# A first norm modulated by columns from strip products, with the load list reordered

## The chip, the cores and the metric

The kernel runs on one core of one Trainium2 chip. The metric is the device time of one execution in microseconds (us). The core has a TensorE (products), a VectorE, a ScalarE and a GpSimd engine, and SyncE, whose queue issues the weight loads. Each runs its own instructions in order and waits on semaphores.

## The reference

One sequence of 256 tokens of width 1024 goes through a first block (a modulated hybrid mixer and a mixture of experts) and then two attention layers. Only the beginning matters here:

```python
c_act = jax.nn.silu(c)
mod = (c_act @ w_mod[l] + b_mod[l])[:, None, :]          # 6 x 1024 columns
sh1, sc1, gt1, sh2, sc2, gt2 = jnp.split(mod, N_MOD, axis=-1)
h = layer_norm(x) * (1.0 + sc1) + sh1
proj = h @ w_in                                           # z, xbc, dt, q, k, v, f, g_ssd, g_att
...
xbc = jax.nn.silu(causal_depthwise_conv(xbc, conv_w, conv_b))
dt = jax.nn.softplus((dt_raw + dt_bias).astype(jnp.float32))
log_f = jax.nn.log_sigmoid((f_raw + forget_b).astype(jnp.float32))
```

All data are f32.

## The kernel before, in words

**Chunks and the ring.** Weights come in chunks of 2 MB (128 partitions x 4096 f32) into a ring of three slots. FIRST_CHUNKS lists the chunks of the first block in the order of their loads, and chunk n of the list has slot n mod 3. SyncE (`load`, line 1179) issues them in that order; ahead of each it waits until the last user of the slot has ended (`used`, set where TensorE's product is written), and everything later in the list stands behind that wait. The list begins mod0, mod2, mod1, mod3, dtf, xbc0, xbc1, xbc2, xbc3, q, k, v, z0, z1, ga0, ga1. dtf is small: 24 columns in two loads, 96 KB.

**Modulation.** mod0 and mod1 are the halves of the shift, mod2 and mod3 those of the scale. `modulation(i)` (line 702) makes rows of 512 columns, the same in all 128 partitions. For mod0 and mod2 (in MOD_SUMMED) VectorE multiplies the chunk's eight parts by c_act and adds them up (`add_modulation`, L1794 and L1796), and one product with ones sums over the partitions (L707). For mod1 and mod3 eight products with a broadcast c_act do it all (L713). The bias is added by a one-row product (L719).

**Norm.** VectorE runs the layer norm on rows (L1684 to L1694), takes the modulation from PSUM (`take_modulation`, L1806), scales and shifts the rows h_rows in two halves (L1699, L1701), and TensorE transposes them (`turn_rows`, L586) into the PSUM banks X and O in turns. ScalarE copies each piece twice (L1401): to h_t in f32 and to first_high, a rounded fp32r. VectorE makes first_low, the difference (L1831).

**Split products.** The chunks in FIRST_SPLIT (xbc0 to xbc3, q, k, v, z0, z1, ga0, ga1) are multiplied as three fp32r passes: high x high, high x low, low x high. For each, ScalarE makes the high part (`make_high`, L1353) once the chunk has landed, and VectorE the low part in place (`make_low`, L1669). TensorE waits for the low part. `product_turned` (L626) gives xbc, q and k in two halves in the banks G0 and G1. ScalarE takes them out (`take_first`, L1339) and then makes the high part of the chunk two further on.

**dtf.** Its plain f32 product (`product_rows`, L611) stands before xbc0's. VectorE and ScalarE compute softplus from it in small steps (L1837 to L1867 on VectorE, L1410 to L1413 on ScalarE), and VectorE makes the low part of xbc1 only after them.

**Order on VectorE after that:** low xbc2, `convolve(0)` (L1881, L1883), low xbc3, `convolve(1)`, low q, `convolve(2)`, low k, low v and so on. On ScalarE the tanh of convolution group i - 1 (`conv_gate`, L1407) follows the high part that is made after xbc i.

## Time and profile before

| what | value |
|---|---|
| three timed runs | 1970.43, 1972.98, 1973.97 us; median 1972.98 |
| the profiled execution | 1971.96 us, its span (first to last instruction) 1970.2 us |
| TensorE products, busy | 1755.8 us, 89% of the span |
| VectorE, ScalarE, GpSimd busy | 853.9, 593.7, 22.6 us |
| TensorE's mean granted clock | 0.932 of full |
| first split product starts | 63.3 us |

Times inside the profile are counted from the first instruction. Engines are PE (TensorE), PEld (its weight loads), DVE (VectorE), ACT (ScalarE), POOL (GpSimd), SP (SyncE), and a name with q is an engine's own queue of issues. L with a number is a line of the kernel, which can be a helper's. In a row of the timeline the first number is the start, the second the time from there to the end of the group, both in us; an entry in brackets says how long the engine was idle before it, and what released it. A plain f32 product is two instructions (passes), an fp32r product one.

### The profile page before, as it was taken

The numbers are of one execution on the slowest core, as the hardware profiler recorded it, in microseconds if no ns is written. First come the engines' busy times: TensorE is split into PE (matmuls) and PEld (weight loads), VectorE is DVE, ScalarE is ACT, GpSimd is POOL, SyncE is SP. The second block draws the span as 40 slices with busy tenths as digits, with TensorE's granted clock in tenths as the row PEclk, the third lists the DMA queues.
The fourth block names the chain that finished last, engine by engine and source line by source line (L and its number), as shares of the span: only waits on it lengthen the run. The fifth ranks groups of instructions, "written<-read, shape, count | busy, mean of one in ns | idle before, by whom it ended". The sixth has DMA issues, their size and how long they took to land.

```text
span 1970.2 us, 21742 instructions
## 1 busy us (share of the span) xinstructions
PE 1755.8 (89%) x9183; PEld 1284.4 (65%) x9183; DVE 853.9 (43%) x1201; ACT 593.7 (30%) x879; POOL 22.6 (1%) x80
## 2 busy tenths in 40 slices
PE   5999899988999959999988779996999989859997
PEld 1997555454434328565677679985756667649995
DVE  4675153243101055353465345534543365434643
ACT  1443210000111123243434234423333533433341
POOL 1000010000000000000000000000000000000000
PEclk9899787988999979999989889997999998979998
DMA  7455222657999964413234135536433232414552
GB/s 242 170 179 201 91 86 85 219 193 292 400 401 405 405 137 165 152 44 128 107 128 171 43 129 172 204 118 151 167 107 110 99 140 105 167 43 154 189 178 90
DMA packets 211212, 333.24 MB, mean 169 GB/s; under 512 B 51251, under 2 KB 102709, under 8 KB 211125
## 3 DMA queue, kind: packets, MB, share of 16 engines
q1 hardware_dynamic: 205312, 325.90, 47.5%
q10 hardware_dynamic: 5814, 6.11, 0.9%
q8 instruction: 65, 1.06, 0.2%
q14 instruction: 21, 0.17, 0.0%
HBM read 330.94 MB, written 1.05 MB: 168 GB/s over the span
## 4 chain that ended last, share of the span: by engine, by line
PE 68%; issue 12%; DVE 8%; DMA 7%; ACT 4%; SPq 1%; POOL 0%; POOLq 0%; DVEq 0%; ACTq 0%
PE ps_g L611 20%; PE ps_g L626 12%; PE ps_g L991 7%; DMA arena<-in_w_up_dram 5%; PE ps_g L911 4%; PE ps_o L681 3%; PE ps_p L611 2%; PE ps_s L611 2%; DMA ring<-in_w_mod_dram 2%; PE ps_p L1128 2%; PE ps_s L1128 2%; PE ps_s L652 1%; DVE ring_r L1669 1%; PE ps_x L586 1%; PE ps_p L671 1%
## 5 line engine op out<-in xcount | busy, mean ns | idle before, releaser
L1669 DVE TENSOR_TENSOR ring_r<-ring,late_w 128x4096 fp32r<-128x4096 f32 (+1 forms) x52 | 225.8, 4343 | 153.5 <-ACT late_w L1353 153.5
L1353 ACT ACTIVATE late_w<-ring 128x4096 fp32r<-128x4096 f32 (+1 forms) x52 | 185.0, 3557 | 234.7 <-PE ps_g L626 111.5
L626 PE MATMUL ps_g<-h_t_r,late_w 128*128 128x256 f32 x768 | 219.0, 285 | 0.0
L626 PE MATMUL ps_g<-hf_high,late_w 128*128 128x256 f32 x704 | 199.0, 283 | 3.8 <-DVE h_t_r L1657 3.8
L626 PE MATMUL ps_g<-hf_high,ring_r 128*128 128x256 f32 x704 | 199.0, 283 | 0.0
L626 PEld LDWEIGHTS ps_g<-h_t_r,late_w 128*128 128x128 f32 x768 | 148.6, 193 | 0.0
L991 PE MATMUL ps_g<-ring,h_t 128*128 128x512 f32 x320 | 145.7, 600 | 0.0
L626 PEld LDWEIGHTS ps_g<-hf_high,late_w 128*128 128x128 f32 x704 | 135.1, 192 | 4.5 <-DVE h_t_r L1657 4.5
L626 PEld LDWEIGHTS ps_g<-hf_high,ring_r 128*128 128x128 f32 x704 | 134.8, 192 | 0.0
L911 PE MATMUL ps_g<-ring,arena 128*64 128x512 f32 x384 | 115.7, 602 | 10.4 <-DMA arena<-in_w_up_dram 8.8
L1339 ACT ACTIVATE arena<-ps_g 128x512 f32<-128x512 f32 (+2 forms) x62 | 35.2, 567 | 219.3 <-PE ps_g L611 145.3
L991 PEld LDWEIGHTS ps_g<-ring,h_t 128*128 128x128 f32 x320 | 58.2, 190 | 63.9 <-issue 62.7
L611 PE MATMUL ps_g<-ring,h_t 128*128 128x512 f32 (+1 forms) x224 | 92.7, 573 | 5.0 <-DVE arena L2031 3.0
L911 PEld LDWEIGHTS ps_g<-ring,arena 128*64 128x64 f32 x384 | 36.5, 139 | 84.1 <-issue 84.1
L1377 ACT ACTIVATE arena<-arena,neg_max 128x256 f32<-128x256 f32 (+1 forms) x160 | 71.3, 448 | 61.0 <-DVE neg_max L1720 61.0
L586 PE MATMUL ps_x<-ident,h_rows 128*128 128x128 f32 x80 | 18.8, 379 | 73.1 <-DVE h_rows L1677 31.5
L611 PE MATMUL ps_g<-ring,arena 128*128 128x512 f32 (+1 forms) x176 | 75.3, 589 | 2.7 <-issue 1.6
L611 PE MATMUL ps_g<-early_w,mix_high 128*128 128x512 f32 (+2 forms) x192 | 72.9, 380 | 5.0 <-issue 5.0
L611 PEld LDWEIGHTS ps_g<-ring,h_t 128*128 128x128 f32 x224 | 43.7, 214 | 49.9 <-issue 48.6
L611 PE MATMUL ps_g<-ring_r,mix_high 128*128 128x512 f32 (+2 forms) x192 | 72.5, 378 | 0.0
L611 PE MATMUL ps_g<-early_w,mix_low 128*128 128x512 f32 (+2 forms) x192 | 72.2, 376 | 0.0
L681 PEld LDWEIGHTS ps_o<-arena 128*128 128x128 f32 x400 | 54.7, 211 | 26.3 <-issue 26.3
(525 smaller groups left out, 3366.6 us busy)
## 6 DMA issues: line engine op xcount, KB each, us to landing
ring<-in_w_in_dram SPq DMA_DIRECT2D x27, 2048.0 KB, 7.8
ring<-in_w_gate_up_dram SPq DMA_DIRECT2D x44, 1024.0 KB, 6.9
ring<-in_w_gate_dram SPq DMA_DIRECT2D x16, 2048.0 KB, 16.5
arena<-in_w_down_dram SPq DMA_DIRECT2D x16, 2048.0 KB, 15.3
ring<-in_w_mod_dram SPq DMA_DIRECT2D x12, 2048.0 KB, 9.4
ring<-in_w_down_dram SPq DMA_DIRECT2D x10, 2048.0 KB, 7.7
ring<-in_w_up_dram SPq DMA_DIRECT2D x8, 2048.0 KB, 18.0
arena<-in_w_up_dram SPq DMA_DIRECT2D x8, 2048.0 KB, 19.3
```

The lines of the kernel that those rows point to most:

```text
L586: ins = pe.transpose(b.ap[0:size, i * SEQ + tb * P:i * SEQ + (tb + 1) * P], piece(tb), ident[:, :])
L611: ins = pe.matmul(b.ap[:, 0:n], x[:, k, tb * P:(tb + 1) * P], a[:, k, lo:lo + n], start=k == 0 and i == 0, stop=k == nk - 1 and i == len(b ...
L626: ins = pe.matmul(b.ap[:, (f % 2) * SEQ:(f % 2 + 1) * SEQ], a[:, k, f * P:(f + 1) * P], x[:, k, :], start=k == 0 and i == 0, stop=k == nk ...
L652: ins = pe.matmul(s4[:, i, 0:nk], q[lo:lo + HD, pair, qb * P:(qb + 1) * P], kk[lo:lo + HD, kpair, 0:nk], start=True, stop=kind != "fox")
L681: ins = pe.matmul(O.ap[:, i * width:(i + 1) * width], probs_t[:, i, b, :], v(step, i, b), start=b == 0, stop=b == kbs - 1)
L911: ins = pe.matmul(b.ap[lanes, :], taken_t[:, k, lanes], w[:, k, :], start=k == 0, stop=k == KD - 1)
L991: ins = pe.matmul(G[tb].ap[:, :], h_t[:, k, tb * P:(tb + 1) * P], w[:, k, :], start=k == 0, stop=k == KD - 1)
L1128: ins = pe.matmul(b.ap[:, half * HALF:(half + 1) * HALF], a[:, k, tb * P:(tb + 1) * P], x[:, k - 4 * c, half * HALF:(half + 1) * HALF], st ...
L1339: act.activation(d, src, func, scale=scale).then_inc(b.free, 1)
L1353: act.activation(high_w[name][:, 0:n], ring[:, slot, 0:n], ACT.Copy).then_inc(high_ready.sem, 1)
L1377: ins = act.activation(s, s, ACT.Exp, bias=neg_max[:, n % 2, i:i + 1], scale=-1.0, accum_out=den[:, n % 4, i:i + 1])
L1669: dve.tensor_tensor(ring_r[:, slot, 0:n], ring[:, slot, 0:n], high_w[name][:, 0:n].bitcast(F32), ALU.subtract).then_inc(low_ready.sem, 1)
```

## The change

The norm's modulation is no longer made as rows. For each of mod0, mod2, mod1 and mod3 eight products (`mod_quarters`) use c_act as a stationary operand of only 32 columns; the product of part k goes to the PSUM partitions of strip k mod 4, so the four strips hold partial sums. ScalarE keeps them in SBUF (`keep_quarters`). One-column products (`mod_columns`) with `quarter`, which has a one in the first partition of each strip, sum the strips and put the result on the partitions; a second one-column product adds the bias. TensorE transposes the normed but unmodulated rows into the banks S and PT, and VectorE scales and shifts them from there into h_t with one instruction for each of eight tiles (`first_columns`). High and low parts of h are made in two halves (`first_rows_high`, `first_rows_low`).

VectorE's sums for mod0 and mod2 are gone. xbc0 is loaded third, ahead of mod1 and mod3; dtf stays sixth in the list. dtf's product goes behind xbc1's, in the banks S and PT; ScalarE's part of softplus goes behind the take of xbc1, and VectorE's behind `convolve(0)`, ahead of the low part of xbc3.

```diff
-MOD_SUMMED = [0, 2, 8, 9, 10, 11]
-FIRST_CHUNKS = (MOD_FIRST + ["dtf"] + [f"xbc{i}" for i in range(4)] + ["q", "k", "v", "z0", "z1", "ga0", "ga1", "mod8", "gs0", "mod9", "att", "gs1",
+MOD_SUMMED = [8, 9, 10, 11]
+FIRST_CHUNKS = (MOD_FIRST[:2] + ["xbc0"] + MOD_FIRST[2:] + ["dtf"] + [f"xbc{i}" for i in range(1, 4)] + ["q", "k", "v", "z0", "z1", "ga0", "ga1", "mod8", "gs0", "mod9", "att", "gs1",
                 "mod4", "so0", "so1", "mod10", "mod5", "o0", "o1", "mod11", "mod6", "mod7"])
...
-        ASIDE = ("bra1", "brb1", "brc1", "out1", "memv", "xo1")
-
-        MOD_ORDER = range(len(MOD_FIRST))
+        ASIDE = ("dtf", "bra1", "brb1", "brc1", "out1", "memv", "xo1")
 
...
-            return (S, PT) if part == "layer" and tag in ASIDE else G
+            return (S, PT) if tag in ASIDE else G
...
-            for i in MOD_ORDER:
-                modulation(i)
+            def mod_quarters(j):
+
+                name, b = MOD_FIRST[j], G[j % 2]
+                w = keys(chunk(pe, "first", name), KD, HALF)
+                claim(b, name)
+                for k in range(KD):
+                    lanes = slice(32 * (k % 4), 32 * (k % 4) + 32)
+                    ins = pe.matmul(b.ap[lanes, :], c_act[:, k:k + 1].broadcast_to([P, 32]), w[:, k, :], start=k < 4, stop=k >= 4)
+                ins.then_inc(b.full, 1)
+                used["first", name] = (b, name)
+
+            def mod_columns(j):
+
+                b, (at_b, name) = G[j % 2], ((X, "mod_left") if j < 2 else (O, "mod_right"))
+                i = int(MOD_FIRST[j][3:])
+                pe.wait_ge(b.free, b.nth("first", MOD_FIRST[j]))
+                if j % 2 == 0:
+                    claim(at_b, name)
+                for k in range(4):
+                    col = at_b.ap[:, 4 * (j % 2) + k:4 * (j % 2) + k + 1]
+                    pe.matmul(col, mod_cols(i)[:, k * P:(k + 1) * P], quarter[:, :], start=True, stop=False)
+                    ins = pe.matmul(col, b_mod[0:1, 0, i * HALF + k * P:i * HALF + (k + 1) * P], tri[0:1, P:P + 1], start=False, stop=True)
+                if j % 2:
+                    ins.then_inc(at_b.full, 1)
+
+            mod_quarters(0)
+            pe.wait_ge(rows.sem, rows.at("first", "h"))
+            for r, b in enumerate((S, PT)):
+                claim(b, f"h{r}")
+                for k in range(4):
+                    for tb in range(TB):
+                        ins = pe.transpose(b.ap[:, k * SEQ + tb * P:k * SEQ + (tb + 1) * P], h_rows[:, tb, (4 * r + k) * P:(4 * r + k + 1) * P], ident[:, :])
+                ins.then_inc(b.full, 1)
+            mod_quarters(1)
+            pe.wait_ge(in_small, 16)
+            mod_columns(0)
+            mod_columns(1)
+            pe.wait_ge(in_stage, 16 * 4)
+            mod_quarters(2)
+            mod_columns(2)
+            mod_quarters(3)
+            mod_columns(3)
...
-            turn_rows("h", [lambda tb, k=k: h_rows[:, tb, k * P:(k + 1) * P] for k in range(KD)],
-                      ready={0: (rows.sem, rows.at("first", "h_left")), 2: (rows.sem, rows.at("first", "h_right"))})
-            turned("first", "h", 4)
-
-
-            w = chunk(pe, "first", "dtf")[:, 0:KD * 24].rearrange("p (k n) -> p k n", n=24)
-            product_rows("first", "dtf", "dtf", h_t, w, KD, 0, 24)
-            pe.wait_ge(first_low_ready, 1)
+            def dt_forget():
+
+                for b in (S, PT):
+                    pe.wait_ge(b.free, b.nth("first", "h0" if b is S else "h1"))
+                w = chunk(pe, "first", "dtf")[:, 0:KD * 24].rearrange("p (k n) -> p k n", n=24)
+                product_rows("first", "dtf", "dtf", h_t, w, KD, 0, 24)
+
+            pe.wait_ge(first_low_ready, 2)
             for name in FIRST_SPLIT:
                 w, x = weights("first", name, KD, HALF), (first_high, first_low)
                 if name in ("v", "z0", "z1", "ga0", "ga1"):
                     product_rows("first", name, name, x, w, KD, 0, HALF)
                 else:
                     product_turned("first", name, name, x, w, KD)
+                if name == "xbc1":
+                    dt_forget()
...
+            st.done(pool.memset(quarter[:, :], 0.0))
+            st.settle()
+            for j in range(4):
+                st.done(pool.memset(quarter[32 * j:32 * j + 1, :], 1.0))
             st.settle()
...
+            def keep_quarters(j):
+
+                b = G[j % 2]
+                act.wait_ge(b.full, b.nth("first", MOD_FIRST[j]))
+                act.activation(mod_cols(int(MOD_FIRST[j][3:])), b.ap[:, :], ACT.Copy).then_inc(b.free, 1)
+
+            def first_rows_high(r):
+
+                b = (S, PT)[r]
+                act.wait_ge(b.free, b.nth("first", f"h{r}"))
+                act.activation(first_high[:, 4 * r:4 * r + 4, :], h_t[:, 4 * r:4 * r + 4, :], ACT.Copy).then_inc(first_high_ready, 1)
+
+            keep_quarters(0)
+            keep_quarters(1)
             make_high("xbc0", 0, part="first")
-            for r in range(4):
-                b = (X, O)[r % 2]
-                act.wait_ge(b.full, b.nth("first", f"h{r}"))
-                for dst in (h_t, first_high):
-                    ins = act.activation(dst[:, 2 * r:2 * r + 2, :], b.ap[:, :].rearrange("p (k n) -> p k n", n=SEQ), ACT.Copy)
-                ins.then_inc(b.free, 1)
-            make_high("xbc1", 0, (rows.sem, rows.at("first", "h_right")), part="first")
+            first_rows_high(0)
+            keep_quarters(2)
+            keep_quarters(3)
+            first_rows_high(1)
+            make_high("xbc1", 0, (O.full, O.nth("first", "mod_right")), part="first")
...
-            act.wait_ge(sp_abs, 1)
-            act.activation(a_log_b[:, :], a_log_b[:, :], ACT.Exp)
-            act.activation(sp[:, 1], sp[:, 1], ACT.Exp, scale=-1.0).then_inc(sp_exp, 1)
-            act.wait_ge(sp_one, 1)
-            act.activation(sp[:, 3], sp[:, 2], ACT.Ln).then_inc(sp_ln, 1)
...
+                if i == 1:
+                    act.wait_ge(sp_abs, 1)
+                    act.activation(a_log_b[:, :], a_log_b[:, :], ACT.Exp)
+                    act.activation(sp[:, 1], sp[:, 1], ACT.Exp, scale=-1.0).then_inc(sp_exp, 1)
+                    act.wait_ge(sp_one, 1)
+                    act.activation(sp[:, 3], sp[:, 2], ACT.Ln).then_inc(sp_ln, 1)
...
-            dve.wait_ge(c_ready, 1)
-            for i in MOD_SUMMED[:2]:
-                add_modulation(i)
             dve.wait_ge(in_x, 16)
             layer_norm("first", "h", x_rows, h_rows)
             layer_norm_end("first", "h", x_rows, h_rows)
-            for half, name in enumerate(("h_left", "h_right")):
-                cols = slice(half * HALF, (half + 1) * HALF)
-                for i in (half, 2 + half):
-                    take_modulation(i)
-                for i in (half, 2 + half):
-                    dve.wait_ge(mod_bank(i).free, mod_bank(i).nth("first", MOD_CHUNKS[i]))
-                scale_shift(h_rows[:, :, cols], mod[:, 1, cols], mod[:, 0, cols]).then_inc(rows.sem, 1)
-
+            dve.sem_inc(rows.sem, 1)
+
+            def first_columns(r):
+
+                at_b, name, b = ((X, "mod_left", S), (O, "mod_right", PT))[r]
+                dve.wait_ge(at_b.full, at_b.nth("first", name))
+                st.done(dve.tensor_copy(mod_col[:, 0, 4 * r:4 * r + 4], at_b.ap[:, 0:4]))
+                dve.tensor_scalar(mod_col[:, 1, 4 * r:4 * r + 4], at_b.ap[:, 4:8], 1.0, None, ALU.add).then_inc(at_b.free, 1)
+                st.settle()
+                dve.wait_ge(at_b.free, at_b.nth("first", name))
+                dve.wait_ge(b.full, b.nth("first", f"h{r}"))
+                for k in range(4 * r, 4 * r + 4):
+                    ins = dve.tensor_scalar(h_t[:, k, :], b.ap[:, (k - 4 * r) * SEQ:(k - 4 * r + 1) * SEQ], mod_col[:, 1, k:k + 1], mod_col[:, 0, k:k + 1],
+                                            ALU.mult, ALU.add)
+                ins.then_inc(b.free, 1)
+
+            def first_rows_low(r):
+
+                for b, i in ((S, 0), (PT, 1)):
+                    dve.wait_ge(b.full, b.nth("first", f"h{i}"))
+                dve.wait_ge(first_high_ready, r + 1)
+                dve.tensor_tensor(first_low[:, 4 * r:4 * r + 4, :], h_t[:, 4 * r:4 * r + 4, :], first_high[:, 4 * r:4 * r + 4, :].bitcast(F32), ALU.subtract)\
+                    .then_inc(first_low_ready, 1)
+
+            first_columns(0)
+            make_low("xbc0", "first")
+            first_rows_low(0)
+            first_columns(1)
+            first_rows_low(1)
...
-            make_low("xbc0", "first")
-            for b, r in ((X, 2), (O, 3)):
-                dve.wait_ge(b.free, b.nth("first", f"h{r}"))
-            dve.tensor_tensor(first_low[:, :, :], h_t[:, :, :], first_high[:, :, :].bitcast(F32), ALU.subtract).then_inc(first_low_ready, 1)
...
-            dve.wait_ge(in_vec, 16 * 7)
-            for tb, b in enumerate(G):
-                dve.wait_ge(b.full, b.nth("first", "dtf"))
-                dve.tensor_tensor(sp[:, 0, tb, :], b.ap[:, 0:24], bias24[:, :], ALU.add).then_inc(b.free, 1)
...
+            def take_dt_forget():
+
+                dve.wait_ge(in_vec, 16 * 7)
+                for tb, b in enumerate((S, PT)):
+                    dve.wait_ge(b.full, b.nth("first", "dtf"))
+                    dve.tensor_tensor(sp[:, 0, tb, :], b.ap[:, 0:24], bias24[:, :], ALU.add).then_inc(b.free, 1)
+                for b in (S, PT):
+                    dve.wait_ge(b.free, b.nth("first", "dtf"))
+                st.done(dve.tensor_scalar(sp[:, 0, :, SSD_HEADS:], sp[:, 0, :, SSD_HEADS:], -1.0, None, ALU.mult))
+                st.settle()
+                dve.scalar_tensor_tensor(sp[:, 1], sp[:, 0], -1.0, sp[:, 0], ALU.mult, ALU.max).then_inc(sp_abs, 1)
+                dve.wait_ge(sp_exp, 1)
+                dve.tensor_scalar(sp[:, 2], sp[:, 1], 1.0, None, ALU.add).then_inc(sp_one, 1)
+                dve.wait_ge(sp_one, 1)
...
+                st.done(dve.scalar_tensor_tensor(sp[:, 5], sp[:, 0], 0.0, sp[:, 3], ALU.max, ALU.add))
+                st.settle()
+                st.done(dve.tensor_copy(dt_a[:, 0], sp[:, 5, :, 0:SSD_HEADS]))
+                st.done(dve.tensor_scalar(sp[:, 5, :, SSD_HEADS:], sp[:, 5, :, SSD_HEADS:], HD ** 0.5, None, ALU.mult))
+                st.settle()
+                dve.scalar_tensor_tensor(dt_a[:, 1], dt_a[:, 0], -1.0, across(a_log_b[:, :], TB), ALU.mult, ALU.mult).then_inc(forget_ready, 1)
 
             make_low("xbc1", "first")
...
             make_low("xbc2", "first")
             convolve(0)
+            take_dt_forget()
             make_low("xbc3", "first")
             convolve(1)
             make_low("q", "first")
```

## Rows read from the trace of the kernel before

**Rows 1.** The page: busy time, share of the span and instructions of the engines.

```profile
PE 1755.8 (89%) x9183; PEld 1284.4 (65%) x9183; DVE 853.9 (43%) x1201; ACT 593.7 (30%) x879; POOL 22.6 (1%) x80
```

**Rows 2.** Chain that ended last, 0 to 200 us: start, us, what.

```profile
26.73 9.43 PE ps_g L713 x16
...
39.32 7.06 PE ps_g L713 x16
...
56.30 6.99 PE ps_g L611 x32
...
63.30 70.67 PE ps_g L626 x576
```

**Rows 3.** Issues in order of time, then issues by tensor (last: us to landing).

```profile
5.34 0.41 ACTq L1315 DMA_DIRECT2D x_rows<-in_x_dram  x1
...
17.22 0.54 SPq L1202 DMA_DIRECT2D ring<-in_w_mod_dram  x1
...
26.73 1.88 SPq L1202 DMA_DIRECT2D ring<-in_w_in_dram  x2
...
47.47 0.37 SPq L1202 DMA_DIRECT2D ring<-in_w_in_dram  x1
...
ring<-in_w_mod_dram SPq DMA_DIRECT2D x1, 2048.0 KB, 15.5
...
x_rows<-in_x_dram ACTq DMA_DIRECT2D x1, 1024.0 KB, 9.0
...
ring<-in_w_in_dram SPq DMA_DIRECT2D x1, 2048.0 KB, 7.7
```

**Rows 4.** Timeline of ScalarE, 64 to 146 us.

```profile
64.44 1.28 ACT L1413 ACT_TABLE_LOAD   x1
...
77.32 0.60 ACT L1339 ACTIVATE arena<-ps_g 128x512 f32<-128x512 f32 x1 [5.05 <-PE ps_g L626]
77.82 3.62 ACT L1353 ACTIVATE first_w<-ring 128x4096 fp32r<-128x4096 f32 x1
...
104.04 1.04 ACT L1407 ACTIVATE arena<-arena 128x1024 f32<-128x1024 f32 x1
...
145.10 0.60 ACT L1339 ACTIVATE arena<-ps_g 128x512 f32<-128x512 f32 x1 [4.95 <-PE ps_g L611]
```

**Rows 5.** Timeline of VectorE, 20 to 93 us.

```profile
20.70 0.49 DVE L1794 TENSOR_SCALAR arena<-ring,c_act 128x512 f32<-128x512 f32 x1 [3.51 <-DMA ring<-in_w_mod_dram]
...
26.61 2.47 DVE L1684 BATCH_NORM_STATS2 bn<-x_rows 128x6 f32<-128x512 f32 x4
...
30.42 1.54 DVE L1694 TENSOR_SCALAR h_rows<-x_rows,mean_var,rstd 128x1024 f32<-128x1024 f32 x2 [0.82 <-POOL rstd L1288]
...
56.31 2.29 DVE L1831 TENSOR_TENSOR first_low<-h_t,first_high 128x2048 fp32r<-128x2048 f32 x1 [1.00 <-ACT first_high L1401]
...
67.19 0.19 DVE L1867 SCALAR_TENSOR_TENSOR dt_a<-dt_a,a_log_b 128x32 f32<-128x32 f32 x1
67.30 4.42 DVE L1669 TENSOR_TENSOR ring_r<-ring,first_w 128x4096 fp32r<-128x4096 f32 x1
...
85.81 1.38 DVE L1881 TENSOR_SCALAR arena<-arena,conv_col 128x256 f32<-128x256 f32 x4
...
87.22 5.09 DVE L1883 SCALAR_TENSOR_TENSOR arena<-arena,conv_col 128x256 f32<-128x256 f32 x12
```

**Rows 6.** Timeline of TensorE: transposes at 53 us, expert products at 500 us.

```profile
53.91 1.12 PE L586 MATMUL ps_o<-ident,h_rows 128*128 128x128 f32 x4
...
500.05 0.59 PE L911 MATMUL ps_g<-ring,arena 128*64 128x512 f32 x1
500.06 0.59 PE L911 MATMUL ps_g<-arena 128*64 128x512 f32 x1
500.48 0.59 PE L911 MATMUL ps_g<-ring,arena 128*64 128x512 f32 x1
```

**Rows 7.** TensorE by stretch: us, busy (x), granted clock, DMA share, GB/s.

```profile
62.00:64.00 2.00, 2.00 (x11) 0.50 0.00 0
```

More of the change, by code:

```diff
@@ L314, in two_blocks @@
         g_col = sb("g_col", [P, G_END])
+        mod_col = sb("mod_col", [P, 2, KD])
+        quarter = sb("quarter", [P, 1])
         neg_max = sb("neg_max", [P, 2, HEADS])
@@ L482, in mod_bank @@
                 return (S, PT)[MOD_SUMMED.index(i) % 2]
-            return G[i // 2 if i < len(MOD_FIRST) else i % 2]
+            return G[i % 2]
         def mod_cols(i):
@@ L528, in two_blocks @@
         gy_ready = sem("gy_ready")
-        rows = Named(sem("rows_ready"), first=(1, ["h_left", "h_right", "gy", "mg", "h2"]),
+        rows = Named(sem("rows_ready"), first=(1, ["h", "gy", "mg", "h2"]),
                      layer=(LAYERS, ["mix", "swa", "nsa", "twice", "lat", "mk", "blk", "hcv", "ob", "mem", "merged", "xattn", "ffn"]))
@@ L714, in modulation @@
                     used["first", name] = (b, name)
-                if i == MOD_ORDER[0]:
-                    pe.wait_ge(in_small, 16)
-                    pe.wait_ge(in_stage, 16 * 4)
-                if i < len(MOD_FIRST):
-                    ins = pe.matmul(b.ap[:, 0:HALF], tri[0:1, P:SEQ], b_mod[0:1, 0, i * HALF:(i + 1) * HALF], start=False, stop=True)
-                else:
-                    for j in range(HALF // P):
-                        row = BIAS_ROW + (i - len(MOD_FIRST)) * (HALF // P) + j
-                        ins = pe.matmul(b.ap[:, j * P:(j + 1) * P], ident[BIAS_ROW:, row:row + 1].broadcast_to([P - BIAS_ROW, P]), stage[BIAS_ROW:, :],
-                                        start=False, stop=j == HALF // P - 1)
@@ L725, in modulation @@
-                ins.then_inc(b.full, 1)
-            for i in MOD_ORDER:
-                modulation(i)
+                for j in range(HALF // P):
+                    row = BIAS_ROW + (i - len(MOD_FIRST)) * (HALF // P) + j
+                    ins = pe.matmul(b.ap[:, j * P:(j + 1) * P], ident[BIAS_ROW:, row:row + 1].broadcast_to([P - BIAS_ROW, P]), stage[BIAS_ROW:, :],
+                                    start=False, stop=j == HALF // P - 1)
+                ins.then_inc(b.full, 1)
+            def mod_quarters(j):
[7 more added lines that the diff above has]
+                used["first", name] = (b, name)
@@ L1838, in _ @@
-            for b in G:
-                dve.wait_ge(b.free, b.nth("first", "dtf"))
-            st.done(dve.tensor_scalar(sp[:, 0, :, SSD_HEADS:], sp[:, 0, :, SSD_HEADS:], -1.0, None, ALU.mult))
-            st.settle()
-            dve.scalar_tensor_tensor(sp[:, 1], sp[:, 0], -1.0, sp[:, 0], ALU.mult, ALU.max).then_inc(sp_abs, 1)
-            dve.wait_ge(sp_exp, 1)
-            dve.tensor_scalar(sp[:, 2], sp[:, 1], 1.0, None, ALU.add).then_inc(sp_one, 1)
-            dve.wait_ge(sp_one, 1)
-            st.done(dve.tensor_scalar(sp[:, 4], sp[:, 2], -1.0, None, ALU.add))
@@ L1866, in _ @@
-            st.settle()
-            dve.scalar_tensor_tensor(dt_a[:, 1], dt_a[:, 0], -1.0, across(a_log_b[:, :], TB), ALU.mult, ALU.mult).then_inc(forget_ready, 1)
+            st.settle()
+            def take_dt_forget():
[11 more added lines that the diff above has]
+                dve.wait_ge(sp_one, 1)
+                st.done(dve.tensor_scalar(sp[:, 4], sp[:, 2], -1.0, None, ALU.add))
+                st.settle()
+                st.done(dve.tensor_scalar(sp[:, 5], sp[:, 4], 0.0, None, ALU.is_equal))
+                st.settle()
+                st.done(dve.tensor_tensor(sp[:, 4], sp[:, 4], sp[:, 5], ALU.add))
+                st.settle()
+                st.done(dve.reciprocal(sp[:, 4], sp[:, 4]))
+                st.done(dve.tensor_tensor(sp[:, 5], sp[:, 5], sp[:, 1], ALU.mult))
+                st.settle()
+                st.done(dve.tensor_tensor(sp[:, 4], sp[:, 4], sp[:, 1], ALU.mult))
+                st.settle()
+                dve.wait_ge(sp_ln, 1)
+                st.done(dve.tensor_tensor(sp[:, 3], sp[:, 3], sp[:, 4], ALU.mult))
+                st.settle()
+                st.done(dve.tensor_tensor(sp[:, 3], sp[:, 3], sp[:, 5], ALU.add))
+                st.settle()
+                st.done(dve.scalar_tensor_tensor(sp[:, 5], sp[:, 0], 0.0, sp[:, 3], ALU.max, ALU.add))
+                st.settle()
+                st.done(dve.tensor_copy(dt_a[:, 0], sp[:, 5, :, 0:SSD_HEADS]))
+                st.done(dve.tensor_scalar(sp[:, 5, :, SSD_HEADS:], sp[:, 5, :, SSD_HEADS:], HD ** 0.5, None, ALU.mult))
+                st.settle()
+                dve.scalar_tensor_tensor(dt_a[:, 1], dt_a[:, 0], -1.0, across(a_log_b[:, :], TB), ALU.mult, ALU.mult).then_inc(forget_ready, 1)
```

21 lines of the change are left out of this document (1 added, 20 removed).

## Prediction, made before the change was run

> **What bounds the kernel now.** I read the page first: TensorE is busy in 89% of the span and no other engine is above half [rows 1]. Then the chain of work that ended last, from the start to 200 us, because the change touches nothing behind the first products. It is a TensorE chain with a load in front: the products of mod1 (from 26.73, when its chunk has landed) and mod3 (39.32), then the turned rows, then dtf's product (56.30, 6.99 us), and from 63.30 six products without a gap in 70.67 us [rows 2]. The sixth product's end is what everything later hangs on: its successors v, z0 and so on follow on the same chain. So the question is how much sooner or later TensorE can start and chain the products xbc0, xbc1, xbc2, xbc3, q.
>
> Third, SyncE's queue, since the change reorders its loads. The ring has three slots, and a load waits for the last user of its slot, with every later load behind it. Before, dtf's two small loads go out at 26.73; xbc1 goes out at 47.47, when mod3's product has ended, and a load issued alone lands 7.7 us later; xbc3, in xbc0's slot, goes out when xbc0's product has ended (77.3) [rows 3, 4]. So xbc1 is in place (about 55.2) eight microseconds before xbc0's product begins. Fourth, ScalarE and VectorE: each weight chunk of the split products needs a "high" copy on ScalarE (3.62 us) and then a "low" difference on VectorE (4.42 us) before TensorE may start on it [rows 4, 5]. xbc0's second half is taken at 77.32, so its product lasted 14.0 us, and each of the five behind it (70.67 - 14.0) / 5 = 11.3 us. The 2.7 us are the clock: it is granted at half (1.2 GHz; 0.50 at 62 to 64 us) after the mostly idle stretch of the turned rows, and rises to full (2.4 GHz) within that product [rows 2, 4, 7].
>
> **Part 1: when xbc0's product starts (now 63.3).** The change takes two runs of vector sums (eight steps each; the second began at 20.70) from in front of the norm, which then began at 26.61 and ended at 31.96 [rows 5]. x lands at about 14.3 (issued 5.34, 9.0 us), so the norm now runs 14.3 to 19.7 [rows 3, 5]. The removed scaling and shifting of rows (mod3's product ends at 47.5, then VectorE, 16 transposes and eight ScalarE copies until 56.2) becomes column sums and eight fused scale-and-shift instructions. By steps:
>
> - mod2's strips. The chunk lands at 20.70 as now. Sixteen transposes come first: 3.6 to 4.4 us by the row of L586 (four in 1.12 us at half clock), 19.7 to about 23.7 [rows 6]. A strip chunk is 16 passes of 512 columns. A full-width pass takes 0.44 us at full clock (16 in 7.06 us), so twice that at half. If four strips run together a chunk costs 16/4 x 0.87 = 3.5 us at half clock and 1.7 us at full; if they run one after another, 14 or 7 us [rows 2]. The nearest row is the expert products: two 64-wide strips begin in the same 0.01 us and the next pair 0.43 us later, the price of one full-width pass [rows 6]. I take together, and keep the serial price for the rivals. End about 27.
>
> - Column sums. For each chunk eight one-column products of two passes. The nearest row is dtf's: 32 passes of 24 columns in 6.99 us at half clock, 0.218 us each [rows 2, 7]. So 3.5 us a chunk at half clock, 1.75 at full; mod0 and mod2 end at 31 to 34. VectorE's two copies and four instructions of 256 (1.38 us for four in the conv row [rows 5]) take about 2 us, ScalarE's half high 1.05.
>
> - mod1's chunk stands fourth in the queue and lands where the fourth lands now, 17.22 + 15.5 = 32.7 [rows 3]; mod3, issued at 27, lands about 5.2 us behind it, 37.9 (2 MB at the pace of a full queue). After it: strips 1.7 to 3.4, ScalarE's copy 0.6, column sums 1.75 to 3.5, VectorE 2.0, high 1.05, low 1.15 (half of L1831's 2.29). With mod1's steps ahead of that this gives a start of xbc0 at 49.5 with everything at full clock, 53.5 at half. The floor is mod3's landing plus these, about 46. I take 51: 12.3 us sooner than now. dtf's 7 us have moved away.
>
> The Trainium skill, TensorEngine Tiling (Array Packing), Instruction Overhead, says a matmul with one column has the latency of one with 60 columns, some 60 cycles. By that an estimate for a chunk's 16 passes is 0.8 us at half clock in place of 3.5, xbc0 would start at about 46.5 and the whole sum come to +19 in place of +23; the row of dtf (24 columns, 0.218 us) speaks against it, since there the weight load of each pass sets the pace. The same page's Overview gives four tiles for outputs up to 32 wide; the trace shows it for two.
>
> **Part 2: the wait that the new load order makes.** By the new list the slots are mod0 0, mod2 1, xbc0 2, mod1 0, mod3 1, dtf 2, xbc1 0, xbc2 1, xbc3 2. So dtf's load waits until xbc0's product has ended, and xbc1 and xbc2, whose slots are long free, stand behind it in SyncE's queue. Call the end of xbc0's product E: 51 + 14.0 = 65.0 (half clock at its start as now, since the steps before it leave TensorE mostly waiting; 62.3 at full clock).
>
> - dtf's two issues take 1.88 us in a full queue, 0.75 at least; its small rows cost perhaps 2 us of the engines; then xbc1's 7.7. It lands at E + 10.6 (bounds 8.5 and 12) [rows 3].
> - high 3.6, low 4.4: xbc1's product starts at E + 18.7. Behind the waiting high copy in ScalarE's queue stand the takes of xbc0; they take 1.2 us while VectorE makes the low, and cost nothing.
> - xbc1's product: 11.3, and 2.2 for the clock, which an 18.7 us idle lowers (bounds 0 and 2.7, the latter from 14.0 against 11.3): E + 32.2.
> - dtf's product, moved here: 32 passes at full clock, half of 6.99: 3.5. E + 35.7. Meanwhile xbc2 is ready (lands 16, high 19.5, low 24), so its product runs 35.7 to 47.0.
>
> **Part 3: the second wait.** xbc3's slot is dtf's, so its load goes out only at E + 35.7, lands at 43.4, and its high copy ends at 47.0. The low copy now stands on VectorE behind the whole softplus of dt, and that needs ScalarE behind the high copy: the tanh of conv group 0 (1.04), Exp and Ln with a table load of 1.28 (some 1.9 in all), then the last six small operations (0.2 each, about 1.4 with their waits) and the low 4.4 [rows 4, 5]: 47.0 + 1.0 + 1.9 + 1.4 + 4.4 = E + 55.7. TensorE is done at 47.0: 8.7 us of idle. In the kernel before the softplus lay beside xbc0's product, and the table load with it. Then xbc3's product with 2.2 for the clock: E + 69.2. q is ready by then: loaded behind xbc3 (48.7), high 54.4, low after convolution 1 (6.5 us) at 66.6.
>
> **The sum.** q's product starts at 65.0 + 69.2 = 134.2; now it starts 34.0 us (three products) after 77.3, at 111.3. The difference is -12.3 + 18.7 + 2.2 + 3.5 + 8.7 + 2.2 = +23.0. From q on each engine's order and each load's slot are as before and hang on TensorE, so it is carried to the end. It costs nothing that the convolution's columns and the quarter's five small GpSimd fills move: they lie under loads. The profiled run took 1971.96 us (span 1970.2), 1.0 below the median of the three runs shown. Forecast: 1971.96 + 23.0 = 1995.
>
> **The rivals.** (a) The strips run one after another: mod2's end at 30, xbc0 starts at about 57, +29, 2001. Against it stand the paired strips; for it, that no row has strips 32 wide. (b) The first wait does not arise, because xbc1 is somehow in place: then 20.9 us fall away, +2.1, 1974. Against it is the queue's order; every load in the trace left in the order of the list. (c) The faster side: both held loads lie under TensorE's work, so that only the earlier start counts (with dtf's 7 us gone from in front of it) and dtf's 3.5 behind xbc1: -12.3 + 3.5 = -8.8, 1963. The place is SyncE's wait in front of dtf's load; it turns the sign if the two waits and their clock (31.8 us here) cost under 8.8. Since load, high and low alone are 15.7 us from the end of xbc0's product, it needs SyncE not to wait for that product. (d) The delay is real but half of it is taken up later: TensorE's next long wait, from v to z0 (145.10 to about 156.7), would have to depend on something other than TensorE; the chain there starts from taking v [rows 4]. About +12, 1984.
>
> **How the numbers follow.** Chances: forecast 0.79, (a) 0.06, (d) 0.06, (b) 0.05, (c) 0.04. The likeliest case's own bounds: start of xbc0 46 to 54 (-5, +3), its clock (-2.7), landing (-2, +1.5), the two clock terms (-4.4, +1), dtf's product at half clock (+3.5 less what the second wait takes back). Not all go one way, so 1985 to 2003, which also holds (a); (b) and (c), just under 1 in 10, lie outside, and (d) at its edge. A change of under 0.2% (3.9 us) can't be told from none. Slower by more is forecast, (a), (d): 0.91; within is (b): 0.05; faster is (c): 0.04.
>
> **What the profile after would show.** Right: dtf's and xbc1's issues just after the last pass of xbc0's product; ScalarE's high of xbc1 released by a load; two gaps of TensorE between the first four products, of about 19 and 9 us; the clock at half behind the first; xbc0's first pass near 51. Wrong: xbc1's issue ahead of xbc0's end, a strip chunk over 6 us, xbc0's start past 57, or the second gap absent because the low of xbc3 does not wait for the softplus.

## The result

The change makes the kernel slower, about as forecast. Its four timed runs are 1993.13 to 2000.8 us, median 1995.43; the kernel before, in its four runs, has a median of 1972.69. The ratio is 1.012, with a 95% interval of 1.0099 to 1.0141. The forecast was 1995, with a range of 1985 to 2003. A second measurement of the unaltered changed kernel (e8_after_again) gave 1994.35 us and 1.0117 (1.01 to 1.0134).

The first view of the profile after is the chain that ended last, from 50 us to v's product (start, us, what; its lines answer to [rows 2]):

```profile
50.82 1.06 ACT first_high L1446
...
52.01 1.24 DVE first_low L1884
...
53.29 13.79 PE ps_g L626 x96
67.09 0.37 SPq L1238
...
67.50 0.58 SPq L1238
...
68.13 8.20 DMA ring<-in_w_in_dram
76.35 3.62 ACT first_w L1393
...
80.07 4.44 DVE ring_r L1721
...
84.55 13.54 PE ps_g L626 x96
98.09 1.70 PE ps_s L611 x16
...
101.60 8.64 DMA ring<-in_w_in_dram
...
110.27 3.63 ACT first_w L1393
...
117.94 4.43 DVE ring_r L1721
...
122.42 36.10 PE ps_g L626 x288
158.52 11.20 PE ps_g L611 x48
```

Before, this stretch was one unbroken TensorE row of 576 passes. Now it is cut in three. xbc0's product starts at 53.29, 10.0 us sooner than before. At its end, 67.08, the chain leaves TensorE for SyncE: only then are dtf's two loads and xbc1's load issued, one behind another. xbc1 lands at 76.3, its high and low parts take 8.1 us, and its product starts at 84.55. dtf's product (3.5 us) ends at 101.6, and there the chain goes to memory a second time, for xbc3's load, whose slot dtf had. v's product (158.52; L611 x48) is the first after q and shows what is carried on: before it started at 133.96, the end of the 70.67 us row [rows 2]. It is 24.6 us late.

TensorE's waits from 50 to 130 us (waiter, releaser: us in total, times, longest) give the two gaps:

```profile
PE ps_g L626 <- DVE ring_r L1721: 26.9, 2, 17.5
```

The longest is 17.5, so the second is 9.4. Last, TensorE's granted clock by stretch, for comparison with [rows 7] (us, busy, granted clock, DMA share, GB/s):

```profile
56.00:58.00 2.00, 2.00 (x12) 0.50 0.00 0
58.00:60.00 2.00, 2.00 (x18) 0.95 0.00 0
...
86.00:88.00 2.00, 2.00 (x11) 0.50 0.00 0
88.00:90.00 2.00, 2.00 (x15) 0.77 0.00 0
```

The granted clock is at half at the start of xbc0's product, as it was before, and again at the start of xbc1's behind the gap. That is why the two products last 13.79 and 13.54 us and not 11.3.

### The profile page after: what moved, and what is told of

It is laid out like the page before. It is cut to its first block, busy times and chain, and to the rows that moved or that the text cites. A ratio compares the mean times of both kernels' runs of the same rounds, so it can differ in the third digit from the quotient of the medians.

```text
span 1995.8 us, 21903 instructions
## 1 busy us (share of the span) xinstructions
PE 1754.0 (88%) x9267; PEld 1289.6 (65%) x9267; DVE 839.9 (42%) x1190; ACT 594.0 (30%) x877; POOL 23.0 (1%) x85
## 3 DMA queue, kind: packets, MB, share of 16 engines
HBM read 330.94 MB, written 1.05 MB: 166 GB/s over the span
## 4 chain that ended last, share of the span: by engine, by line
PE 64%; issue 12%; DVE 8%; DMA 8%; ACT 4%; SPq 1%; POOL 0%; POOLq 0%; DVEq 0%; ACTq 0%
PE ps_g L611 19%; PE ps_g L626 12%; PE ps_g L1027 7%; DMA arena<-in_w_up_dram 6%; PE ps_g L947 4%; PE ps_o L681 3%; PE ps_p L611 2%; PE ps_s L611 2%; DVE ring_r L1721 2%; PE ps_s L1164 2%; PE ps_p L1164 2%; PE ps_s L652 2%; PE ps_p L671 1%; PE ps_x L586 1%; PE ps_s L912 1%
## 5 line engine op out<-in xcount | busy, mean ns | idle before, releaser
L1027 PE MATMUL ps_g<-ring,h_t 128*128 128x512 f32 x320 | 145.7, 600 | 0.0
L947 PE MATMUL ps_g<-ring,arena 128*64 128x512 f32 x384 | 115.7, 602 | 13.8 <-DMA arena<-in_w_up_dram 12.3
L1027 PEld LDWEIGHTS ps_g<-ring,h_t 128*128 128x128 f32 x320 | 58.2, 190 | 63.9 <-issue 62.7
L611 PE MATMUL ps_g<-ring,h_t 128*128 128x512 f32 x192 | 84.5, 597 | 3.3 <-DVE arena L2099 2.6
L626 PE MATMUL ps_g<-first_high,first_w 128*128 128x256 f32 x192 | 57.2, 298 | 31.3 <-DVE ring_r L1721 26.9
L611 PE MATMUL ps_g<-ring,arena 128*128 128x512 f32 (+1 forms) x176 | 74.7, 585 | 2.7 <-issue 1.6
L611 PE MATMUL ps_g<-early_w,mix_high 128*128 128x512 f32 (+2 forms) x192 | 72.5, 377 | 5.0 <-issue 5.0
L611 PE MATMUL ps_g<-ring_r,mix_high 128*128 128x512 f32 (+2 forms) x192 | 72.4, 377 | 0.0
L611 PE MATMUL ps_g<-early_w,mix_low 128*128 128x512 f32 (+2 forms) x192 | 71.6, 373 | 0.0
## 6 DMA issues: line engine op xcount, KB each, us to landing
ring<-in_w_up_dram SPq DMA_DIRECT2D x8, 2048.0 KB, 18.3
arena<-in_w_up_dram SPq DMA_DIRECT2D x8, 2048.0 KB, 19.8
```

Source lines behind the costliest of these rows:

```text
L611: ins = pe.matmul(b.ap[:, 0:n], x[:, k, tb * P:(tb + 1) * P], a[:, k, lo:lo + n], start=k == 0 and i == 0, stop=k == nk - 1 and i == len(b ...
L626: ins = pe.matmul(b.ap[:, (f % 2) * SEQ:(f % 2 + 1) * SEQ], a[:, k, f * P:(f + 1) * P], x[:, k, :], start=k == 0 and i == 0, stop=k == nk ...
L947: ins = pe.matmul(b.ap[lanes, :], taken_t[:, k, lanes], w[:, k, :], start=k == 0, stop=k == KD - 1)
L1027: ins = pe.matmul(G[tb].ap[:, :], h_t[:, k, tb * P:(tb + 1) * P], w[:, k, :], start=k == 0, stop=k == KD - 1)
```

## The experiments

All comparisons of totals are with the kernel before on the same chip. Beside each total stands the start of v's product in the profile (before 133.96, changed 158.52), since that is the first point behind everything that the change touches, and since the totals scatter (see the end of this section). That start scatters too, by about 1 us. The column sums of mod1 met the half clock in some profiles (4.1 us in the changed kernel's) and the full clock in others (2.5 us in its second profile, e8_after_again), and xbc0's product starts at 53.2 to 53.6 in the former (changed, e2, e5) and at 52.0 to 52.2 in the latter (e1, e3, e8). The first and most used edit takes dtf out of the ring, into the idle area of gate_ssd (cut here: the landing counts without dtf, and TensorE's wait for `in_dtf` ahead of dtf's product):

```diff
+        dtf_w = view(at, KD, 24)
...
             def load(part, name, rnd=0):
+                if name == "dtf":
+                    for cols, piece in zip((dtf_w[:, :, 0:SSD_HEADS], dtf_w[:, :, SSD_HEADS:]), sources(part, name, rnd)):
+                        sync.dma_start(cols, piece).then_inc(in_dtf, 16)
+                    return
```

**Both waits taken away (e1_dtf_apart).** The edit above.

> The changed kernel with one thing different: dtf's two small loads go to a place of their own outside the ring (in the idle area of gate_ssd) and wait for nothing. Its turn in the list stays, so all other slots are the same. xbc1 and xbc2 are then issued once mod1 and mod3 are used, and xbc3 once xbc0's product has ended. My theory (both gaps are the load queue's): xbc0 still starts at about 53 us, xbc1 follows it without a gap at 67, dtf's product 78.4 to 81.9, xbc2 to 93.2, xbc3 without a gap to 104.5, where the kernel before has 111.3: about 6.8 us faster than before, 1966 us, ratio 0.9966; against the changed kernel 29 us less. Rival 1 (the strips, columns and the new order on VectorE cost the time themselves): xbc1's product still starts late and the time stays above 1980. Rival 2 (only the first gap is the queue's, the second is the softplus on VectorE): a gap of 5 to 9 us ahead of xbc3, about 1973.

Measured: 1964.56 us against 1969.71, ratio 0.998 (0.9964 to 0.9996). The chain:

```profile
52.20 25.79 PE ps_g L627 x192
77.99 1.70 PE ps_s L612 x16
...
81.47 46.94 PE ps_g L627 x384
128.41 11.20 PE ps_g L612 x48
```

TensorE does not wait from xbc0 to k (dtf's product is the piece from 77.99 to 81.47). v's product starts 5.5 us sooner than before, and 30.1 us sooner than in the changed kernel; the median of the total is 5.1 below before. Rival 1 falls (the strips, the columns and the new order on VectorE are all in this kernel), and so does rival 2. The forecast was 6.8. What is missing lies mainly in the row from 81.47: its four products take 46.94 us in place of 45.3. The clock shows why, though TensorE is busy all the time:

```profile
78.00:82.00 4.00, 4.00 (x38) 1.00 0.74 229
82.00:84.00 2.00, 2.00 (x13) 0.57 1.05 408
84.00:86.00 2.00, 2.00 (x13) 0.58 0.51 187
```

It fell right behind dtf's product of 24-column passes (78.0 to 81.5).

**The second wait alone (e2_second_kept).** The same with `last[PLACE[part, name][0]] = (part, name, rnd)` ahead of the return, so that xbc3's load still waits for dtf's product.

> As the run with dtf outside the ring, but SyncE still holds xbc3's load until dtf's product has ended, as in the changed kernel. This keeps the second wait alone. My theory: no gap ahead of xbc1 and xbc2; xbc3 is issued at 81.9, lands at 90, its low part is ready at 102.6 and TensorE idles 9.4 us; q's product starts at about 115.9 against 111.3 in the kernel before: 4 to 5 us slower than before, about 1977, ratio 1.002. Rival (the second wait is the softplus ahead of the low part, not the load): the same time as the run without the held load. Rival (the first wait was worth nothing): still about 1995.

Measured: 1979.89 us, ratio 1.0054 (1.0036 to 1.0073). The chain:

```profile
53.17 25.52 PE ps_g L627 x192
...
82.20 8.55 DMA ring<-in_w_in_dram
90.77 3.63 ACT first_w L1399
...
98.45 4.43 DVE ring_r L1727
102.92 35.94 PE ps_g L627 x288
138.86 11.20 PE ps_g L612 x48
```

There is no gap ahead of xbc1. xbc3's product starts 20.7 us behind the end of dtf's (82.20 to 102.92), as in the changed kernel (20.8). TensorE idles 7.8 us of that and not 9.4, because here xbc2's product met a stretch at half clock (0.50 from 84 to 86 us), which the wait hides. v starts 4.9 us later than before, as expected (4 to 5); the total is 10.2 later, twice that. With the held load gone in the first experiment the gap was gone too, although the softplus stood in the same place: so the held load makes the gap, and the softplus and the tanh only lengthen it (90.77 + 3.63 = 94.4 to 98.45, 4.0 us).

**The first wait alone (e5_first_kept).** dtf outside the ring, with `sync.wait_ge` for the end of xbc0's product ahead of its loads.

> dtf outside the ring as in the first experiment, but SyncE still waits for the end of xbc0's product ahead of dtf's loads. This keeps the first wait alone: xbc1, xbc2 and xbc3 are all issued behind it, and xbc3 no longer waits for dtf's product. My theory: a gap of 17.4 us ahead of xbc1 as in the changed kernel (67 to 84.5), no gap ahead of xbc3, q's product at about 124 (67.1 + 57.2) against 134.9 in the changed kernel and 111.4 in the kernel before; v's product at about 147; about 13 us slower than before, 1983 us, ratio 1.0065. Rival (the two waits are one: without the first there is no second, and with the first the second comes anyway): a gap of 9 us ahead of xbc3 and the time of the changed kernel.

Measured: 1989.89 us, ratio 1.0103 (1.0084 to 1.0122). The chain:

```profile
53.55 14.35 PE ps_g L627 x96
...
68.95 8.14 DMA ring<-in_w_in_dram
...
85.32 13.87 PE ps_g L627 x96
...
102.67 45.53 PE ps_g L627 x384
148.21 11.20 PE ps_g L612 x48
```

One gap, ahead of xbc1, of 17.4 us (67.90 to 85.32), and none ahead of xbc3: the two waits are separate. v starts 14.25 us later than before (expected: about 147, so 13); again the total has moved further, by 18.3.

**The softplus behind the low part (e3_low_first).**

```diff
-            take_dt_forget()
             make_low("xbc3", "first")
+            take_dt_forget()
```

> The changed kernel with the low part of xbc3 ahead of the softplus on VectorE, nothing else. The low part then ends at 118.3 in place of 122.4. My theory: TensorE does not gain the 4.1 us, because xbc3's product also needs the bank G0, and ScalarE takes xbc2 out of it only behind the Ln, which now waits for VectorE behind the low part: the product starts at about 120.9, 1.5 us sooner, and the time is about 1994, ratio 1.011. Rival (the low part is all that counts): start at 118.4, 1991.5. Rival (the softplus is late for something behind it): no gain or a loss.

Measured: 1998.25 us, ratio 1.0161 (1.0137 to 1.0184). The chain:

```profile
117.69 1.28 ACT L1476
...
119.86 36.82 PE ps_g L626 x288
```

xbc3's product is now released by ScalarE, which takes xbc2 out of its bank behind the table load of the Ln, not by the low part. The fair comparison is the second profile of the changed kernel, where xbc0 starts within 0.12 us of here: xbc3's product starts 1.6 us sooner (119.86 against 121.45), where 1.5 was expected and 4.1 would have been the naive gain, and v's 0.95 sooner (156.67 against 157.62), since the three products between take 36.82 us and not 36.18. The total does not show it: it lies 28.5 us above before and the changed kernel's 22.7, with an interval that only touches the changed kernel's. With four runs of it and the scatter below I draw nothing from that.

**No strips (e4_full_width).**

```diff
-                    lanes = slice(32 * (k % 4), 32 * (k % 4) + 32)
-                    ins = pe.matmul(b.ap[lanes, :], c_act[:, k:k + 1].broadcast_to([P, 32]), w[:, k, :], start=k < 4, stop=k >= 4)
+                    ins = pe.matmul(b.ap[:, :], c_act[:, k:k + 1].broadcast_to([P, P]), w[:, k, :], start=k == 0, stop=k == KD - 1)
```

> The changed kernel with full-width products in place of the four strips: each product of the modulation has 128 columns and all eight parts add up in one bank; the column sums then take the first partition alone. The result is the same. My theory (four strips run together, so a chunk costs a quarter): each chunk's 16 passes take 6.9 us at full clock in place of 1.9 to 3.6; xbc0's product starts at about 62 in place of 53.3, 8.5 us later, of which a clock that stays up may give back 2; the time is 2001 to 2004, ratio 1.015 to 1.016. Rival (the wait for mod1's and mod3's chunks or the column products bound this stretch): under 3 us later, 1995 to 1998.

Measured: 2012.95 us, ratio 1.0236 (1.0211 to 1.026). xbc0's product starts at 62.99 (62 expected) and v's at 167.44, 8.9 us behind the changed kernel. In the timeline of TensorE, mod1's and mod3's products here, and under them mod2's and mod1's in the changed kernel (each 16 passes):

```profile
35.51 9.18 PE L727 MATMUL ps_g<-ring,c_act 128*128 128x512 f32 x16
47.86 7.13 PE L727 MATMUL ps_g<-ring,c_act 128*128 128x512 f32 x16
```

```profile
24.20 1.92 PE L728 MATMUL ps_g<-ring,c_act 128*32 128x512 f32 x16
...
33.30 3.64 PE L728 MATMUL ps_g<-ring,c_act 128*32 128x512 f32 x16 [2.17 <-issue]
```

Sixteen passes take 7.13 us at full clock at full width and 1.92 in strips, a factor of 3.7: four strips run together. The total, though, lies 43.2 us above before, where the changed kernel's lies 22.7 above: some 20 us more, twice what the stage gives.

**dtf's product in front again (e6_dtf_front).** The first experiment with `dt_forget()` ahead of the split products.

> dtf outside the ring as in the first experiment, and its product back in front of xbc0's. My theory (a product of 24 columns is paid at the clock of its place: 7.0 us in front, where the clock is at half, 3.5 behind xbc1): xbc0's product starts 7 us later than there (59 against 52), the low clock still meets xbc0, nothing is lost behind xbc1 (there the four products behind dtf took 46.9 us in place of 45.3), and v's product starts at about 130.3 against 128.4: 2 us slower than the first experiment, 3.5 faster than before, ratio 0.9985. Rival (dtf's product warms the clock for xbc0): xbc0 takes 11.3 in place of 14 and the move was worth nothing: v's product at 127.5.

Measured: 1966.89 us against 1971.61, ratio 0.9978 (0.9965 to 0.9992); v at 128.07, where the first experiment had 128.41 and 130.3 was expected. dtf's product began at 49.41 and not at 52, because it needs h only in f32 and runs while the low part is made; and it left no clock dip among the later products. It did not warm the clock: with TensorE busy, 50 to 60 us are all at 0.50. Against that the softplus, still ahead of xbc3's low part, cost a wait of 1.4 us ahead of xbc3. The move of dtf's product is worth nothing that these profiles can show (0.3 us at v), for another reason than the rival's.

**The bias in a strip (e7_bias_in_strip).** dtf outside the ring, and:

```diff
+                ins = pe.matmul(b.ap[0:32, :], tri[0:1, P:P + 32], b_mod[0:1, 0, i * HALF:(i + 1) * HALF], start=False, stop=True)
...
-                    pe.matmul(col, mod_cols(i)[:, k * P:(k + 1) * P], quarter[:, :], start=True, stop=False)
-                    ins = pe.matmul(col, b_mod[0:1, 0, i * HALF + k * P:i * HALF + (k + 1) * P], tri[0:1, P:P + 1], start=False, stop=True)
+                    ins = pe.matmul(col, mod_cols(i)[:, k * P:(k + 1) * P], quarter[:, :], start=True, stop=True)
```

> dtf outside the ring as in the first experiment, and the bias added by one one-row product of 512 columns into strip 0, so that the column sums are four one-column products for a chunk in place of eight. My theory (a one-column pass costs its weight load and not its column, 0.155 us at full and 0.26 at half clock): the sums of a chunk halve (2.5 to 1.25 us at full clock, 4.1 to 2.05 at half), the extra product costs up to 0.9 us beside the others. mod0's and mod2's sums lie under the wait for mod1's chunk; on the path are mod1's and mod3's, but mod3's chunk lands at about 40 and hides mod1's. xbc0's product starts at about 50.5 against 52.2 to 53.3, v's at about 126.5, 7 us faster than before, ratio 0.9965. Rival (the chunks' landings bound all of it): same as the first experiment. Rival (the one-row product breaks the strips' overlap): up to 2 us later.

Measured: 1964.36 us against 1971.61, ratio 0.9964 (0.9949 to 0.9978), with xbc0 at 50.10 and v at 126.47, both as expected. It is 7 us faster than the kernel before, the lowest ratio of the versions tried, though its interval overlaps those of the first experiment, of dtf's product in front, and of the next one. mod1's column sums (eight passes; mod3's take the same) in its timeline, with the start of mod3's strips behind them:

```profile
38.07 1.05 PE L746 MATMUL ps_o<-quarter,arena 128*128 128x1 f32 x8 [0.69 <-ACT arena L1447]
39.05 3.22 PE L729 MATMUL ps_g<-ring,c_act 128*32 128x512 f32 x16
```

Of the 2.1 us by which xbc0 starts sooner than in the first experiment, 1.1 are there before the sums begin: mod1's strips start at 32.93 and not at 34.07, which this edit does not explain. The other 1.0 lies on the path that the edit shortens. mod3's strips follow mod1's sums at once, so mod3's chunk hid nothing of them, against the expectation.

**Both (e9_front_and_bias).** The last kernel with dtf's product in front and the softplus beside xbc0's product.

> The kernel with the bias in the strip and dtf outside the ring, and in it dtf's product back in front of xbc0's with the softplus beside xbc0's product, as in the kernel before. My theory: dtf's product needs only h in f32 and begins while the low part is still made, at about 46.3; it ends at 53.3 at half clock, xbc0 (13.0) at 66.3, and five products of 11.3 follow without a gap, since neither the softplus stands ahead of xbc3's low part nor a product of 24 columns lets the clock fall among them: v's product at 123.0 against 126.5 for the bias alone and 134.0 before, 11 us faster than before, 1961 us, ratio 0.9945. Rival (the place of dtf's product is worth nothing either way, as the run with dtf in front gave): 126.5 and 0.9964 again.

Measured: 1964.85 us against 1971.88, ratio 0.9973 (0.9959 to 0.9988). The expectation of 123.0 for v was wrong, and the rival's right:

```profile
50.27 3.58 PE ps_s L612 x16
...
57.27 70.39 PE ps_g L627 x576
127.66 11.20 PE ps_g L612 x48
```

The unbroken row came about, but it started late. h was ready at 50.2 (47.6 with the bias alone), 2.6 us later. mod1's strips started 0.7 us later (33.59 against 32.93), the one-row product of the bias behind them took 0.9 more (1.91 against 1.04) and mod1's sums 0.8 more (1.87 against 1.05), these two because the clock was at half there; small terms make the rest. And I had set dtf's start 3.8 us ahead of xbc0's, where the high and low parts that it runs beside are 2.5.

**The changed kernel again (e8_after_again).**

> The changed kernel, unaltered, on the same chip as the others of this set. My theory: the two gaps of 17.4 and 9.5 us ahead of xbc1 and xbc3 again, v's product within 1 us of 158.5, and the total 20 to 28 us above before, depending on the clock granted between v's product and the experts (in the profiles so far 0.89 to 0.92, 288 to 299 us for the same work). Rival (the spread of the totals comes from the changed part): v's product moves by several us from profile to profile.

Measured: 1994.35 us, ratio 1.0117 (1.01 to 1.0134); gaps of 17.4 and 9.4 us, v at 157.62. v's start repeats within a microsecond (0.9), xbc0's within 1.2.

**The scatter of the totals.** From v's product to the experts' first load every kernel does the same work. This stretch in the profiles of before, the first experiment and the second (stretch, us, TensorE busy, granted clock, DMA share, GB/s):

```profile
134.00:426.60 292.60, 273.59 (x976) 0.90 0.39 137
```

```profile
128.40:416.10 287.70, 268.98 (x977) 0.92 0.40 139
```

```profile
138.90:437.40 298.50, 277.37 (x976) 0.89 0.38 134
```

Ten microseconds of spread go with a granted clock of 0.92 to 0.89. No change of the kernel is needed for a part of it: in its two profiles the unaltered changed kernel took 291.5 us at 0.91 and 294.7 at 0.90. So a single total can't resolve a term of a few microseconds, and I judge those by v's start. Whether the spread has a part that belongs to some kernels stays open: with one wait kept (either one), with the low part first and without strips the medians lie 4 to 10 us above what v's start says, in the others within 2, and no run was made to tell a cause from chance.

## Why the prediction was right, step by step

The term table, from the chain of the changed kernel and [rows 2]:

| term | forecast | measured |
|---|---|---|
| xbc0's product starts | 51 (-12.3) | 53.29 (-10.0) |
| its duration | 14.0 | 13.79 |
| gap ahead of xbc1 | 18.7 | 17.5 |
| xbc1's product above 11.3 | 2.2 | 2.2 |
| dtf's product behind it | 3.5 | 3.5 |
| gap ahead of xbc3 | 8.7 | 9.4 |
| clock behind it | 2.2 | 2.1 (36.10 for three, against 34.0) |
| sum at v's product | +23.0 | +24.6 |

**The load queue.** This was the step that decided, and the waits' and chain's rows show it as forecast: dtf's issue at 67.09, in the same instant in which xbc0's product ended. Each wait was tested alone. By v's start the first is worth 148.21 - 128.41 = 19.8 us (gap and clock), the second 138.86 - 128.41 = 10.5, together 30.3; the changed kernel lies 30.1 behind the version without either. That the sum agrees so closely is in part luck: each of these figures holds a microsecond by which xbc0 happened to start later than in the first experiment. Counted from xbc0's own start the waits are worth 18.5 and 9.5, together 28.0, and the changed kernel lies 29.0 behind; the clock dip behind dtf, which cost the first experiment 1.6 us and is not in every profile, is larger than what is left.

The gap ahead of xbc1 was 17.5 and not 18.7, because xbc1 landed 9.25 us behind xbc0's end (67.08 to 76.33) and not 10.6: dtf's issues and rows cost less than I allowed for them.

**The early start** was over-estimated by 2.3 us, and the working behind it has a slip. Its own terms, added from mod1's landing at 32.7, give 51.9 with everything at half clock; from mod3's at 37.9 they give 46.2 with everything at full. The 53.5 and 49.5 in the text do not come out of them. With the clock that the trace shows (half up to mod3's strips, full for mod3's sums) the terms give 50.2, and 53.29 was measured, 3.1 more. The mis-sized term is the column sums, 1.65 of the 3.1: the two chunks' sums were put at 3.5 and 1.75 us and took 4.1 and 2.8. The rest is mod1's strips, which began at 33.3 and not 32.7, and the small steps between the engines. I took 0.109 us at full and 0.218 at half clock for a pass from dtf's row; two passes measured 0.31 and 0.51 us from start to start:

```profile
37.65 0.59 PE L741 MATMUL ps_o<-quarter,arena 128*128 128x1 f32 x2 [0.70 <-ACT arena L1440]
38.17 0.58 PE L742 MATMUL ps_o<-tri,arena 1*128 1x1 f32 x2
...
45.77 0.38 PE L741 MATMUL ps_o<-quarter,arena 128*128 128x1 f32 x2 [0.73 <-ACT arena L1440]
46.08 0.38 PE L742 MATMUL ps_o<-tri,arena 1*128 1x1 f32 x2
```

So a chunk's 16 passes cost 4.1 us at half and 2.5 at full, for 3.5 and 1.75. The rows with the bias in a strip show what is dear about them. Without the one-row products between, eight one-column passes take 0.98 us at full clock (38.07 to 39.05), 0.12 us each, and 1.80 at half (39.76 to 41.56 in e9_front_and_bias), 0.225 each: nearly the price that I took from dtf's row. It is the alternation of 128-row and one-row products that measured 0.155 and 0.26.

The Trainium skill, TensorEngine Tiling (Array Packing), Instruction Overhead, gives a one-column matmul the latency of one with 60 columns, some 60 cycles. The estimate from it, 0.8 us for the 16 passes at half clock, was further off than mine; the measured 4.1 us (1.80 for eight passes without the one-row products) decide against it for f32 passes with a 128-column weight load each.

**The strips.** I took them as running together, and together they run: 16 passes in 1.92 us, against 7.13 at full width. The Trainium skill, TensorEngine Tiling (Array Packing), Overview, gives a tiling factor of four for a dimension of up to 32, and up to 4x the speed; the trace agrees, with 3.7.

**The second gap** came out in size, 9.4 for 8.7; the difference is the load of xbc3, 8.64 us for 7.7. The inner parts behind it were not as I had them: I counted the tanh, 1.9 us for Exp and Ln and 1.4 for the last small operations, 4.3 in all. VectorE went on at the end of the Exp and ran its own operations from 115.11 to 117.94; ScalarE's table load and the Ln (115.09 to 116.6) lay beside them, and the sum is 4.0. The softplus as such was not the cause, as the first experiment showed.

**The rivals.** (a), (b) and (c) are refuted by the strips' row and the two gaps. (d), that half of the delay is taken up later, is refuted too: the wait of TensorE from v to z0 is 11.6 us in both kernels (145.07 to 156.67 before, 169.72 to 181.33 after), and v's delay of 24.6 us arrives at the end as 22.7 in the medians, a difference that the scatter covers.

**What was luck.** The mechanism, both waits and their order were forecast. That the total came within half a microsecond (+22.7 for +23.0) was not: v's start was off by 1.6 us, made of terms that missed by +2.3, -1.2, +0.7 and less, and the scatter took the rest back.

## What to carry to other kernels

In a ring of slots the load list is a queue: a chunk that is used late holds its slot, and what waits for that slot holds every load behind it, also those whose slots are free. When a list is reordered, write the slot beside each name and ask for each load who used the slot last and when; here a 96 KB chunk behind xbc0 cost 28 us of the total (30 at v's start), and giving it a place outside the ring turned a loss of 1.2% into a gain of 0.2%, and of 0.4% with the bias in a strip as well. And price an added wait at the whole chain behind it (issue, landing, two preparing passes, the clock), not at the load.

## What the runs showed of the hardware that was not expected

Behind dtf's 3.5 us of 24-column passes the granted clock fell in some profiles while TensorE was busy all the time. In the first experiment it was 0.57 and 0.58 for 4 us. With the bias in a strip it fell already within dtf's product and was at half for longer, so that four products took 48.06 us. With the second wait alone (0.50 from 84 to 86 us) and without strips (0.50 from 112 to 114) it fell too, hidden under a wait. In the two profiles of the changed kernel, with the low part first and with the first wait alone (45.53 us for four) it did not fall. So it is not tied to the kernel's order alone, and no run here tells what decides it. With the bias in a strip, TensorE by stretch:

```profile
78.00:80.00 2.00, 2.00 (x10) 0.50 1.06 411
...
82.00:84.00 2.00, 2.00 (x11) 0.52 0.03 11
84.00:86.00 2.00, 2.00 (x19) 1.00 0.00 0
```

One-column passes cost about as much as passes of 24 columns (0.12 us against 0.109 at full clock, each with a 128-column weight load), and more, 0.155, where they alternate with one-row products.
